# A two-layer diffusion backbone on one core: the heads' common rotary key is made in the Fourier block, and the second attention begins in another order

## The chip, the cores and the metric

The kernel runs on one core of a Trainium2 chip. The metric is the device time of one execution in microseconds (us). Before the change three runs took 3230.91, 3232.22 and 3234.19 us; the median is 3232.22 us. The core has five engines that work side by side: TensorE (PE, matmuls), VectorE (DVE), ScalarE (ACT), GpSimd (POOL) and SyncE (SP, which here issues all DMA transfers). Each runs its own list of instructions in order; they wait for each other through semaphores.

## The reference, cut to what matters

1024 latent tokens and 256 context tokens of width 1024 go through two layers. Layer 0 mixes tokens by a latent attention beside a Fourier mixing, layer 1 by a windowed attention beside pooling; each layer ends in a gated feed-forward part. The change touches the two attentions only.

```
# layer 0: 12 heads; a key is 64 own numbers and 32 that all heads share
kv = (rmsnorm(ckv, ckv_g) @ w_ukv).reshape(B, L, 12, 64 + 64)
k  = concat([kv[..., :64], broadcast(k_rope[:, :, None, :])])   # k_rope: 32 rows, common to the heads
k  = rope_tail(rmsnorm(k, k_g), cos, sin)                       # rotation of the last 32
o  = latent_dense_attention(q, k, v, k_ctx, v_ctx, scale)
y  = concat([o, fourier_mix(h[..., A_IN:], w_f)]) @ w_out
# layer 1: 12 query heads in 4 groups, one key head per group, window of +-128, context keys in full
q = apply_rope(rmsnorm(q, q_g)); k = apply_rope(rmsnorm(k, k_g))   # the context keys are not rotated
o = window_attention(q, k, v, k_ctx, v_ctx, sink, scale)
```

## The kernel before, in words

Everything is kept transposed: features on the 128 partitions, the 1280 tokens (1024 latent, then 256 context) along the free axis, worked in chunks of 512, 512 and 256 (`CH`). The program is a row of blocks; at the end of a block all engines meet, and the next one starts together. No scheduler reorders anything: the order on each engine is that of the code.

**The Fourier block** (`latents_and_fourier`, L1396 to L1574). SP loads the Fourier tables and the value weights (L1419 to L1422). ACT and PE make the norms of the latents (L1436 to L1444, L1468), DVE makes the sums and differences of the Fourier input (L1537, L1539) and scales the latents (L1557, three instructions). PE then does the short Fourier stage (L1482 to L1495), waits for L1557 (`u` 3 at L1500), does the long one (L1504, L1505), some small pieces (L1508 to L1521), and 20 products for the values (L1530), which ACT takes out of the accumulation memory PS one by one (L1452).

**The first attention** (`heads0`, L1576 to L2113) begins with a preparation that only depends on things that the Fourier block has. SP loads the rotation table `rope` (L1684) into two tiles of `H` that held the Fourier input, and the first two heads' weights (L1688). POOL clears the rows 0 to 63 of the scratch `sk` (L1701), clears the unused rows 96 to 127 of eight operand buffers (L1704: `kh`, `kl`, `qh`, `ql`, two of each), sets a row of ones in each `kh` (L1707) and copies the first head's values (L1712). The common rotary key: ACT copies its 32 rows into `sk` (L2003), PE multiplies them with the rotation matrix (L1897), DVE scales the key by the table (L2088), multiplies PE's result by the other half of the table (L2092) and adds the two into `kx` (L2095), and ACT squares the key for the norms (L2006). PE's list waits for the table, for L2095 and for L2006 before head 0 is prepared: project (L1818, L1822), squares (L1834), norm (L1940, L1943 on ACT, L2027 on DVE), split into a high and a low half (L1951, L2061), cast (L1720 on POOL), row maxima (L1863, L2077) and the row of negated maxima (L1874, L1965). Then the scores of head 0 start (L1750), and from there on each head's preparation is woven into the head before it.

**The second attention** (`heads1`, L2232 to L2862) goes through five products per group of heads (`prods`: which of the two operand tiles and which chunk of tokens). Each product runs through these kinds of steps, placed in slots by `plan`: `sq` (ACT L2668), `nt` (PE L2593, L2595; ACT L2680, L2683), `tn` and `ro` (DVE, L2779, L2801 to L2807, or L2795 alone for a context chunk), `hi` (ACT L2692), `lo` (DVE L2815), `ca` (POOL L2500, the cast to bf16). `upfront` lays out the first four products, before any head. After `hi`, `lo` and `ca` SP moves pieces to the partitions where the matmuls want them (L2465 for the high half, L2471 for the cast one, L2474 for the low half). The row maxima of the first head (PE L2613 to L2618, DVE L2825, 8 of them) wait for the moved casts of three products, then come L2832, L2628 and the row copy L2697, and then the first scores (L2541). POOL's list begins with 13 clearings of unused rows (L2485 to L2491), SP's product loop waits for all of them, and so do POOL's casts.

## Time and profile before

| what | value |
|---|---|
| median of three runs | 3232.22 us |
| the profiled execution | 3230.8 us |
| its span | 3229.0 us |
| PE busy | 3072.0 us, 95% of the span |
| DVE, ACT, POOL busy | 50%, 33%, 15% |
| HBM traffic over the span | 50 GB/s |

The span runs from the first to the last instruction in the trace. All other times below are read from the same execution, in us from the start of the span. A row of the timeline gives the start, the duration, the engine, the line and the operation, then what is written and read; "x4" means four instructions of one kind put in one row, and a bracket behind it gives how long the engine was idle before and what released it. In the rows by stretch, PEclk is the clock that TensorE was granted as a share of 2.4 GHz (0.50 is 1.2 GHz).

### The profile page before, as it was taken

To read this page: it belongs to the slowest core of one execution; us is meant where nothing else is said; L and a number is where in the kernel's file an instruction comes from. 1 tells how busy PE (TensorE), PEld (TensorE's weight loads), DVE (VectorE), ACT (ScalarE), POOL (GpSimd) and SP (SyncE) were. 2 spreads that over 40 slices of the span, in tenths; PEclk is the share of its full clock that TensorE was granted. 3 is DMA by queue.
4 is the path that set the end of the run, shared out by engine and by line. 5 is a ranking of instruction groups with operands and counts; after the bars stand their busy time and mean duration, and the time that the engine had idled before them with its cause. 6 is when DMAs were issued, how large, how long until landed. Compare 5 with 4: busy or idle time off the path is not lost. (4 is left out here: it accounts for less than half of the span.)

```text
span 3229.0 us, 38657 instructions
## 1 busy us (share of the span) xinstructions
PE 3072.0 (95%) x14498; PEld 2201.1 (68%) x14498; DVE 1625.8 (50%) x2090; ACT 1062.7 (33%) x1519; POOL 479.9 (15%) x369
## 2 busy tenths in 40 slices
PE   5987999999999999999999998969999999999999
PEld 2553444444488888888888886844457788888887
DVE  5123556556436544555444456246654655554555
ACT  3013665665624211121222223026652322212221
POOL 0002555555600000000000010034540000000000
PEclk9997999999999999999999999989999999999999
DMA  9910000000031011101111101123211111111111
GB/s 377 365 38 17 4 3 3 3 2 2 7 117 47 33 39 39 39 32 39 39 39 39 39 14 40 39 62 75 58 41 46 60 46 50 61 39 45 45 60 57
DMA packets 49668, 177.68 MB, mean 55 GB/s; under 512 B 6354, under 2 KB 15826, under 8 KB 39763
## 3 DMA queue, kind: packets, MB, share of 16 engines
q1 hardware_dynamic: 49586, 176.59, 16.1%
q8 instruction: 52, 0.85, 0.1%
q14 instruction: 30, 0.24, 0.0%
HBM read 156.77 MB, written 4.19 MB: 50 GB/s over the span
## 5 line engine op out<-in xcount | busy, mean ns | idle before, releaser
L1022 PE MATMUL PS<-s_uh,f_Wh 128*128 128x512 f32 (+1 forms) x1760 | 493.6, 371 | 7.6 <-PEq L134 5.4
L1022 PE MATMUL PS<-s_uh,f_Wl 128*128 128x512 f32 (+1 forms) x1760 | 492.1, 370 | 0.0
L1022 PE MATMUL PS<-s_ul,f_Wh 128*128 128x512 f32 (+1 forms) x1760 | 491.8, 370 | 0.0
L1277 DVE SCALAR_TENSOR_TENSOR X<-PS,mod,X 128x512 f32<-128x512 f32 (+1 forms) x440 | 304.4, 697 | 288.5 <-PE PS L1022 288.3
L1022 PEld LDWEIGHTS PS<-s_uh,f_Wh 128*128 128x128 f32 x1760 | 309.4, 188 | 69.2 <-issue 6.2
L1022 PEld LDWEIGHTS PS<-s_ul,f_Wh 128*128 128x128 f32 x1760 | 309.5, 188 | 58.5 <-issue 0.2
L1022 PEld LDWEIGHTS PS<-s_uh,f_Wl 128*128 128x128 f32 x1760 | 309.3, 188 | 58.7
L1022 PE MATMUL PS<-f_gh,f_WDh 128*128 128x512 f32 (+1 forms) x880 | 329.8, 375 | 8.6 <-DVE X L1277 4.5
L1022 PE MATMUL PS<-f_gl,f_WDh 128*128 128x512 f32 (+1 forms) x880 | 324.6, 369 | 0.0
L1022 PE MATMUL PS<-f_gh,f_WDl 128*128 128x512 f32 (+1 forms) x880 | 324.5, 369 | 0.0
L1248 DVE SCALAR_TENSOR_TENSOR part<-PS,part,part 128x1023 f32<-128x1023 f32 (+1 forms) x129 | 127.0, 1012 | 290.5 <-ACT part L1148 290.4
L1155 ACT ACTIVATE part<-part 128x1280 f32<-128x1280 f32 (+1 forms) x44 | 51.4, 1168 | 621.8 <-DVE part L1255 621.8
L1148 ACT ACTIVATE part<-PS,part 128x1024 f32<-128x1024 f32 (+1 forms) x87 | 113.3, 1303 | 385.3 <-PE PS L1022 385.3
L1730 POOL TENSOR_TENSOR X<-X 128x1024 f32<-128x1024 f32 x96 | 229.5, 2390 | 59.6 <-ACT X L1974 58.7
L1022 PEld LDWEIGHTS PS<-f_gh,f_WDh 128*128 128x128 f32 x880 | 166.3, 189 | 42.9 <-DVE X L1277 8.8
L1974 ACT ACTIVATE X<-PS 128x512 f32<-128x512 f32 x252 | 146.1, 594 | 143.0 <-PE PS L1752 134.8
L1022 PEld LDWEIGHTS PS<-f_gl,f_WDh 128*128 128x128 f32 x880 | 166.6, 189 | 27.8 <-issue 0.2
L1022 PEld LDWEIGHTS PS<-f_gh,f_WDl 128*128 128x128 f32 x880 | 166.4, 189 | 27.4
L2077 DVE TENSOR_REDUCE part<-PS 128x1 f32<-128x512 f32 (+1 forms) x312 | 161.9, 580 | 13.9 <-PE PS L1863 13.1
L509 POOL TENSOR_TENSOR part<-part,part 128x512 f32<-128x512 f32 x7 | 9.4, 1338 | 1037.6 <-ACT part L499 1036.9
L1236 DVE TENSOR_TENSOR f_Wl<-part,f_Wh 128x1024 fp32r<-128x1024 f32 x85 | 103.9, 1222 | 98.4 <-ACT f_Wh L1137 98.4
L1781 PE MATMUL PS<-X,part 128*64 128x512 f32 x480 | 138.1, 614 | 0.0
(289 smaller groups left out, 4669.4 us busy)
## 6 DMA issues: line engine op xcount, KB each, us to landing
part<-in_mod_w SPq DMA_DIRECT2D x48, 1024.0 KB, 7.3
part<-in_w_up SPq DMA_DIRECT2D x88, 512.0 KB, 3.6
part<-in_w_down SPq DMA_DIRECT2D x22, 1024.0 KB, 5.5
part<-in_w_in SPq DMA_DIRECT2D x16, 512.0 KB, 4.7
part<-in_w_out SPq DMA_DIRECT2D x16, 512.0 KB, 3.6
h_qh<-h_stage_h SPq DMA_DIRECT2D x48, 128.0 KB, 2.4
X<-in_xT SPq DMA_DIRECT2D x4, 1280.0 KB, 9.6
X<-in_xT SPq DMA_DIRECT2D x8, 640.0 KB, 8.8
```

Source lines behind the costliest of these rows:

```text
L509: dve.tensor_tensor(self.acc[:, lo:hi], self.acc[:, lo:hi], self.sq[i % 2][:, lo:hi], ALU.add)\
L1022: mm = pe.matmul(ps(bank, x_.shape[-1]), w_, x_, start=first and p_ == 0, stop=final and p_ == 2)
L1148: op = act.activation((cg, cv)[kind][:, lo:hi], hidden(before, place, lo, hi), ACT.Identity, scale=cw[:, ds(f, 1), 1], bias=cw[:, ds(f, 1) ...
L1155: act.activation(sg[:, :], cg[:, :], ACT.Silu).then_inc(s["silu"], 1)
L1236: dve.tensor_tensor(Wl[place % 2][:, :, :], W[place % 2][:, :, :], Wh[place % 2][:, :, :].bitcast(F32), ALU.subtract).then_inc(s["lo"], 1)
L1248: op = dve.scalar_tensor_tensor(out=x[:, lo + 1:hi], in0=h[:, 0:hi - lo - 1], scalar=cw[:, ds(f, 1), 0], in1=x[:, lo + 1:hi], op0=ALU.mult ...
L1277: dve.scalar_tensor_tensor(out=X[:, m, lo:hi], in0=ps(bank, hi - lo), scalar=moda(layer, 5, m, 0 if lo < SEQ else 1), in1=X[:, m, lo:hi], ...
L1730: op = pool.tensor_tensor(ac[:, 0:SEQ], ac[:, 0:SEQ], p[:, :], ALU.add)
L1781: mm = pe.matmul(ps(OB, BANK, slice(64 * c, 64 * c + 64)), vs[b][:, u, :], p[:, c * BANK:(c + 1) * BANK], start=(u == 0), stop=(u == 9))
L1974: act.activation(pr[u % 3][:, i % 2 * BANK:i % 2 * BANK + BANK], ps(i % 3, BANK), ACT.Exp, scale=A_SCALE).then_inc(s["P"], 1)
L2077: dve.reduce_max(mc[:, r:r + 1], ps(MB[c], hi - lo), AX_X).then_inc(s["mc"], 1)
```

## The change

Four things are changed, all in the two attentions and the Fourier block.

1. The common rotary key is made in the Fourier block. SP loads the table there, once the Fourier input in `H` is used up (after the two waits for `eo` and `ab`), and issues the first two heads' weights; POOL clears `sk` there; ACT's copy and square, PE's rotation and DVE's products stand there, the products cut into a latent and a context piece, since PE now writes banks 6, 7 and 4. PE waits for the result (`krc`) before the context pieces and before the value products.
2. The clearing of unused rows for the first attention is split: POOL does the four buffers of head 0 and one row of ones, DVE the four of head 1 and the other one, at the start of DVE's list.
3. In the second attention, the context chunk is the second product of a group instead of the third, and `upfront` puts a product's `hi`, `lo` and `ca` right behind its `ro`, ahead of the next product's norms. Three of the eight row maxima of the first head stand ahead of the fourth product's `ro`, and wait for the casts of two products only.
4. POOL clears the five bf16 buffers first, and the others between its casts; SP's loop no longer waits for the clearings.

```diff
 # Fourier block
+ sp: for b in range(2): sp.dma_start(WQ[b], a["wqk0"][b:b + 1]...).then_inc(loaded[b], 16)
+     sp.wait_ge(s["eo"], 6)
+     sp.wait_ge(s["ab"], 7)
+     sp.dma_start(ROPE[0:A_QK], a["rope0"]).then_inc(s["tab"], 16)
+ act: act.activation(SK[64:96, :], H[0:32, 3, :], ACT.Copy).then_inc(s["kr"], 1)
+      act.wait_ge(s["krm"], 1)
+      act.wait_ge(s["krt"], 1)
+      act.activation(SK[64:96, :], H[0:32, 3, :], ACT.Square).then_inc(s["krs"], 1)
  pe:  pe.wait_ge(s["abc"], 7)
       pe.wait_ge(s["u"], 3)
+      for lo, hi in CH:
+          bank = 6 + lo // BANK if lo < SEQ else 4
+          mm = pe.matmul(ps(bank, hi - lo, slice(0, A_QK)), rot0[:, 1, :], SK[0:A_QK, lo:hi], ...)
       pe.wait_ge(s["df"], 32)
...
+      pe.wait_ge(s["krc"], 2)        # ahead of the context pieces, and again ahead of the values
 # first attention
  pool:
-     pool.memset(sk[0:64, :], 0.0).then_inc(s["zero"], 1)
-     for n, x in enumerate((*kh, *kl, *qh, *ql)):
+     for n, x in enumerate((kh[0], kl[0], qh[0], ql[0])):
+ dve: for n, x in enumerate((kh[1], kl[1], qh[1], ql[1])):
+          dve.memset(x[96:P, :].bitcast(F32), 0.0).then_inc(s["pad1"], 1)
+      dve.wait_ge(s["pad1"], 4)
+      dve.memset(kh[1][96:97, :].bitcast(F32), 1.0).then_inc(s["one1"], 1)
 # second attention
-     prods = [(0, 0), (0, 1), (0, 2), (1, 0), (1, 1)]
+     prods = [(0, 0), (0, 2), (0, 1), (1, 0), (1, 1)]
+     def piece(w, *after):
+         for kind, v in after + (("ro", w),) + (("tn", w + 1),) * (w < 3) + (("hi", w), ("lo", w), ("ca", w)):
+             at(UPFRONT, 0, kind, 0, v)
+     for w in range(3):
+         piece(w, ("sq", w + 1))
+         at(UPFRONT, 0, "nt", 0, w + 1)
+     first(range(3))
+     piece(3)
+     first(range(3, 8))
  sp:
-     sp.wait_ge(s["one"], 2 + QS)
...
-     if q > 1:
+     if q > 0:
          sp.wait_ge(s["rounded"], rounded(q + 1))
+     if q > 1:
          sp.wait_ge(s["moved"], moved(q + 1))
```

How the lists of the engines stand, before and after. First PE. Before, its list goes from the last pieces of the Fourier block over the block's end (the two branches) to the rotation of the common key:

```order
L1521 MATMUL PS<-part_1159,part_1154 128x256 x8
L1530 MATMUL PS<-part_1150,part_58 128x384 x20
L1411 UNCONDITIONAL_BRANCH
L1746 UNCONDITIONAL_BRANCH
L1897 MATMUL PS<-X,rot 96x512 x2
L1897 MATMUL PS<-X,rot 96x256
L1818 MATMUL PS<-part_58,part_1444 64x512 x2
L1834 MATMUL PS<-X,cst 96x512
```

After, the rotation (now L1523) stands in the Fourier block, behind the short Fourier stage (L1513 is its last piece) and ahead of the long one (L1529, L1530):

```order
L1507 MATMUL PS<-part_1155,part_58 128x256 x4
L1513 MATMUL PS<-part_1155,part_58 1x128 x2
L1523 MATMUL PS<-X,rot 96x512 x2
L1523 MATMUL PS<-X,rot 96x256
L1529 MATMUL PS<-part_1159,part_1156 128x512
L1530 MATMUL PS<-part_1159,part_1156 128x512
```

Three matmuls have moved past the long Fourier stage, the context pieces and the values; the first attention's list now begins with the first projections.

Second, VectorE around the same block's end. Before, `L1557` are the latents' scalings, `L1566` to `L1573` the Fourier results, then the block's end, the key (L2088 to L2095), and head 0's first product:

```order
L1557 SCALAR_TENSOR_TENSOR part_58<-part_58,sml,PS 128x1280 x3
L1566 TENSOR_TENSOR part_57<-PS,part_1156 128x512
...
L1411 UNCONDITIONAL_BRANCH
L2018 UNCONDITIONAL_BRANCH
L2088 SCALAR_TENSOR_TENSOR X<-X,sml,part_58 32x1280
L2092 TENSOR_TENSOR PS<-PS,part_58 32x1280
L2095 TENSOR_TENSOR X<-X,PS 32x1280
L2027 TENSOR_TENSOR PS<-X,PS 96x512
```

After, the same key work is L1590 to L1600, head 0's first product is L2045:

```order
L1590 SCALAR_TENSOR_TENSOR X<-X,sml,part_58 32x1280
L1595 TENSOR_TENSOR PS<-PS,part_58 32x1024
L1595 TENSOR_TENSOR PS<-PS,part_58 32x256
L1600 TENSOR_TENSOR X<-X,PS 32x1024
L1600 TENSOR_TENSOR X<-X,PS 32x256
...
L2036 UNCONDITIONAL_BRANCH
L2104 MEMSET h_kh_1471 32x1280
L2104 MEMSET h_kl_1473 32x1280
L2104 MEMSET h_qh_1467 32x1280
L2104 MEMSET h_ql_1469 32x1280
L2106 MEMSET h_kh_1471 1x1280
L2045 TENSOR_TENSOR PS<-X,PS 96x512
```

The key is behind the scalings, and five clearings stand ahead of head 0's first product.

Third, ScalarE at the start of the second attention (L2668 squares, L2680 and L2683 the inverse norm, L2692 the high half, which releases the cast, L2697 the row). Before:

```order
L2668 ACTIVATE part_7876<-part_7876 128x2x256
L2680 ACTIVATE X<-PS,eps 128x2x256
L2683 ACTIVATE PS<-X 128x512
L2668 ACTIVATE part_9015<-part_7876 128x512
L2680 ACTIVATE X<-PS,eps 128x2x256
L2683 ACTIVATE PS<-X 128x512
L2692 ACTIVATE h_stage_h_9026<-PS 128x512
L2668 ACTIVATE part_7876<-part_7876 128x256
L2680 ACTIVATE X<-PS,eps 128x256
L2683 ACTIVATE PS<-X 128x256
L2692 ACTIVATE h_stage_h_9028<-PS 128x512
```

After (L2709, L2721 with L2724, L2733):

```order
L2709 ACTIVATE part_7873<-part_7873 128x2x256
L2721 ACTIVATE X<-PS,eps 128x2x256
L2724 ACTIVATE PS<-X 128x512
L2709 ACTIVATE part_9012<-part_7873 128x256
L2733 ACTIVATE h_stage_h_9023<-PS 128x512
L2721 ACTIVATE X<-PS,eps 128x256
L2724 ACTIVATE PS<-X 128x256
L2709 ACTIVATE part_7873<-part_7873 128x2x256
L2733 ACTIVATE h_stage_h_9025<-PS 128x256
L2721 ACTIVATE X<-PS,eps 128x2x256
```

The first high half stands ahead of the second product's inverse norm, and the second product is the short one.

## Rows read from the trace of the kernel before

**Rows 1.** The page: busy time, share of the span and instructions of an engine.

```profile
PE 3072.0 (95%) x14498; PEld 2201.1 (68%) x14498; DVE 1625.8 (50%) x2090; ACT 1062.7 (33%) x1519; POOL 479.9 (15%) x369
```

**Rows 2.** Stretches: length, then busy PE, PEld, DVE, ACT, POOL; PEclk, DMA share, GB/s.

```profile
221.40:226.70 5.30, 5.25 (x6) 2.19 (x7) 0.00 (x0) 0.00 (x0) 0.00 (x0) 0.50 0.00 0
268.20:288.20 20.00, 13.52 (x17) 3.94 (x18) 5.73 (x5) 6.00 (x11) 10.82 (x11) 0.50 0.14 34
289.00:302.00 13.00, 8.89 (x25) 3.35 (x23) 8.46 (x13) 8.24 (x18) 1.62 (x3) 1.00 0.04 11
2119.40:2155.70 36.30, 17.64 (x52) 6.97 (x52) 19.49 (x28) 10.25 (x18) 15.26 (x17) 0.67 0.44 112
2160.00:2395.00 235.00, 222.82 (x1303) 109.91 (x1301) 144.12 (x192) 144.84 (x259) 123.45 (x117) 0.99 0.25 57
```

**Rows 3.** Timeline: the Fourier block's end, the first attention's start.

```profile
264.27 0.49 ACT L1452 ACTIVATE part<-PS 128x384 f32<-128x384 f32 x1 [0.16 <-PE PS L1530]
265.01 0.33 SPq L1684 DMA_DIRECT2D part<-in_rope  x1
...
271.50 4.58 PE L1897 MATMUL PS<-X,rot 96*96 96x512 f32 x6 [7.26 <-DMA part<-in_rope]
...
276.12 1.50 DVE L2092 TENSOR_TENSOR PS<-PS,part 32x1280 f32<-32x1280 f32 x1 [3.10 <-PE PS L1897]
277.72 1.49 DVE L2095 TENSOR_TENSOR X<-X,PS 32x1280 f32<-32x1280 f32 x1
...
279.26 3.68 PE L1818 MATMUL PS<-part,part 128*64 128x512 f32 x4 [3.18 <-DVE X L2095]
...
286.34 0.69 DVE L2027 TENSOR_TENSOR PS<-X,PS 96x512 f32<-96x512 f32 x1 [7.13 <-ACT PS L1943]
```

**Rows 4.** Timeline: the Fourier block's middle.

```profile
215.86 0.60 PE L1495 MATMUL PS<-part,part 128*1 128x128 f32 x4
...
216.91 4.44 DVE L1557 SCALAR_TENSOR_TENSOR part<-part,sml,PS 128x1280 f32<-128x1280 f32 x3
...
221.45 2.05 PE L1504 MATMUL PS<-part,part 128*128 128x512 f32 x2 [4.99 <-issue]
...
240.87 0.69 DVE L1566 TENSOR_TENSOR part<-PS,part 128x512 f32<-128x512 f32 x1 [19.52 <-ACT part L1448]
```

**Rows 5.** POOL's clearings, grouped, 265 to 280 us: count, busy us, mean ns.

```profile
L1704 POOL MEMSET h_kh<- 32x1280 f32 x2 | 2.3, 1160 | 0.1
```

**Rows 6.** DMA issues: count, KB each, median us from issue to landing.

```profile
part<-in_rope SPq DMA_DIRECT2D x1, 960.0 KB, 6.4
part<-part SPq DMA_DIRECT2D x4, 64.0 KB, 2.0
```

**Rows 7.** Timeline: the second attention's start.

```profile
2124.94 0.70 DVE L2807 TENSOR_TENSOR PS<-X,PS 128x512 f32<-128x512 f32 x1
...
2128.26 0.69 ACT L2680 ACTIVATE X<-PS,eps 128x512 f32<-128x512 f32 x1 [3.87 <-PE PS L2595]
2128.90 3.62 POOL L2491 MEMSET h_ql<- 64x1024 f32 x4
...
2129.52 0.58 ACT L2692 ACTIVATE h_stage_h<-PS 128x512 fp32r<-128x512 f32 x1
...
2134.08 2.07 PE L2593 MATMUL PS<-part,cst 128*128 128x512 f32 x2 [2.93 <-ACT part L2668]
...
2137.89 0.69 ACT L2680 ACTIVATE X<-PS,eps 128x512 f32<-128x512 f32 x1 [3.87 <-PE PS L2595]
...
2144.06 0.54 SPq L2471 DMA_DIRECT2D part<-part  x1
...
2145.93 0.40 PE L2613 MATMUL PS<-part,part 128*128 128x256 bf16 x1 [8.07 <-DMA part<-part]
...
2155.79 0.77 PE L2541 MATMUL PS<-h_qh,h_ks 128*128 128x512 f32 x1 [1.15 <-issue]
```

**Rows 8.** DVE's part of the first head's maxima, grouped, 2145.5 to 2154 us.

```profile
L2825 DVE TENSOR_REDUCE part<-PS 128x1 f32<-128x640 f32 (+1 forms) x8 | 6.2, 790 | 3.4 <-PE PS L2618 3.3
```

More of the change, by code:

```diff
@@ L1591, in heads0 @@
             vs = [take(10, 64) for _ in range(2)]
-            wq = [take(256) for _ in range(2)]
-            Xf = X[:, :, :].rearrange("p k n -> p (k n)")
+            assert o == O_A + 8 * T + 20 * 64
+            o += 512
+            wq = WQ
             acc = [Xf[:, n * T:(n + 1) * T] for n in range(2)]
@@ L1596, in heads0 @@
             rest = 2 * T + 6 * BANK
-            kx, sk = [Xf[:, rest + n * T:rest + (n + 1) * T] for n in range(2)]
+            kx, sk = KX, SK
             rest += 2 * T
@@ L2114, in program @@
         input_and_mods(norm00, u0, copy_take(H, T))
-        latents_and_fourier()
+        loaded = [sem(f"h0_w{b}") for b in range(2)]
+        latents_and_fourier(loaded)
         source0 = Source("out0_", 0, a["w_out0"], T, MIX, [k * T for k in range(KT)],
@@ L2322, in plan @@
                 for jj, r in enumerate((-8, -2, 4)):
[L2323 to L2324 removed]
+                    if (G, jj) == (0, 0):
+                        continue
+                    if (G, jj) == (0, 1):
+                        maxima(G, jj, EARLY, 4)
                     else:
@@ L2518, in casts, with keys, queries_pad @@
                                 cast(*what)
-                    casts(UPFRONT, 0)
+                    def keys(b):
+                        pool.memset(kh[b][64:P, :].bitcast(F32), 0.0).then_inc(s["zero"], 1)
+                        pool.wait_ge(s["zero"], b + 1)
+                        pool.memset(kh[b][64:65, :].bitcast(F32), 1.0).then_inc(s["one"], 1)
+                    def queries_pad(n):
+                        pool.memset(ql[n][64:P, :].bitcast(F32), 0.0).then_inc(s["one"], 1)
+                    for x in (kb[0], qb[2], qb[0], qb[1], kb[1]):
+                        pool.memset(x[64:P, :], 0.0).then_inc(s["pad"], 1)
+                    pool.wait_ge(s["pad"], 2 + C_GROUP)
+                    for kind, *what in steps(UPFRONT, 0):
+                        if kind == "ca":
+                            w = what[1]
+                            cast(*what)
+                            pool.wait_ge(s["cast"], w + 1)
+                            if w == 0:
+                                keys(0)
+                            elif w < 3:
+                                queries_pad(w - 1)
+                            if w < 3:
+                                pool.wait_ge(s["one"], w + 1)
+                    queries_pad(2)
+                    queries_pad(3)
+                    keys(1)
+                    pool.wait_ge(s["one"], 2 + QS)
+                    pool.wait_ge(s["pad"], 2 + C_GROUP)
                     for n in range(C_HEADS):
```

123 lines of the change are left out of this document (58 added, 65 removed).

## The prediction, written before the changed kernel ran

> **What bounds the kernel now.** I read the page first: PE is busy for 3072.0 us, 95% of the span [rows 1]. So a change that only shifts work between the other engines is worth something only where PE stands still, and what is worth reading is the stretches in which it does. The busy times by stretch give two of them that the change touches. From 268.2 to 288.2 us PE is busy for 13.5 of 20.0 us, and at half clock; from 2119.4 to 2155.7 us for 17.6 of 36.3 us [rows 2]. The body of the second attention has PE busy for 222.8 of 235.0 us [rows 2], little to win. Then I read the timeline of both stretches for what PE waits for.
>
> *The first attention's start.* The last value product is taken out by ACT at 264.27 us for 0.49 us, and SP issues the rotation table at 265.01 us [rows 3]. The table holds 960 KB and lands 6.4 us later [rows 6]. The rotation on PE waits for it, 7.26 us idle, until 271.50 us, and takes 4.58 us; then DVE's L2092 and L2095 take 1.50 and 1.49 us in sequence, and PE's first projection starts at 279.26 us, after another 3.18 us idle [rows 3]. From the block's start to the first projection are 279.26 - 265.01 = 14.25 us in which nothing of head 0 is done.
>
> *The second attention's start.* PE is last idle for 8.07 us, released at 2145.93 us by the DMA of the third product's cast, issued at 2144.06 us; the first scores start at 2155.79 us [rows 7]. The first product is finished by DVE at 2124.94 + 0.70 = 2125.64 us, but ACT makes its high half only at 2129.52 us, since the second product's inverse norm (2128.26 us) stands before it in ACT's list; and POOL, which casts it, is clearing buffers until 2128.90 + 3.62 = 2132.52 us [rows 7]. So everything that is moved is some 7 us late from the first product on.
>
> **Part 1: the key moves (saves 14.1, costs 2.2).** What goes: with the key and the weights ready, PE projects at once when the block starts. It starts when SP does, 265.01 us, plus about 0.1 us for the first wait; the gap that goes is 279.26 - 265.15 = 14.1 us.
>
> What comes into the Fourier block, engine by engine:
> - PE: three matmuls between the short and the long stage, after the wait for DVE's scalings, which ends at 221.45 us [rows 4]. In the first attention the same three take 4.58 us, at half clock [rows 2, 3]. Here the clock is also 0.50 from 221.4 to 226.7 us, while PE is fully busy [rows 2]; after 5.3 us of work it is back at full speed. I take that this slow time stays as long, so that the long stage has its slow part shortened by what the rotation takes of it. Then the three cost what they do at full clock, half of about 4.3 us: 2.2 us. The bounds are 0 (hidden, if PE had waited for something later anyway; nothing shows it) and 4.6 us (the slow time starts anew).
> - SP: the table can be issued when the short stage has used up its input, at 215.86 + 0.60 = 216.5 us [rows 4]; plus 6.4 us it lands at 222.9 us. The two weight loads go out behind the Fourier tables and are not wanted before 265 us.
> - DVE: behind the scalings (216.91 + 4.44 = 221.35 us) it now waits for the table, then scales, and from 226 us, when PE's rotation is out, does the products: 1.5 + 1.5 + 1.5 us, and some 0.2 us for the two cuts. It is done by 230 us. What is queued behind is L1566 at 240.87 us, before which DVE is idle for 19.52 us [rows 4]. Hidden with 10 us to spare.
> - ACT: copy and square are 1.3 us each and lie in the same idle time; POOL has nothing else. Nothing.
> - The waits for `krc` on PE, ahead of the context pieces and the values, are past by 230 us.
>
> So 14.1 - 2.2 = 11.9 us.
>
> **Part 2: clearings split between POOL and DVE (about even).** POOL's clearings are 1160 ns each [rows 5]. Four, then a row of ones, and head 0's values: POOL is done with the four 4.8 us after the block's start, in time for the first high half, which comes 7.8 us after the first projection before (286.34 + 0.7 - 279.26). The five on DVE are new and ahead of its first product L2027. No such DVE clearing is in this trace. Bounds: nothing, if they are short; above, the 1.50 us of L2092 over the same 32 x 1280 elements [rows 3], times five, 7.5 us. The nearest row is POOL's 1.16 us; I take 1.3 us, 6.5 us in all, DVE free some 6.6 us after the start. L2027 was wanted 286.34 - 279.26 = 7.1 us after the first projection. But PE now projects and squares at full clock, having been busy until just before, where the first projection and the first squares ran at 0.50 [rows 2]: that brings L2027 forward by about 1.7 us, to 5.4 us. The clearings hold it until 6.6 us. What remains of the clock's gain is 0.5 us. With both bounds the term is +1.7 us (gain) to -0.4 us.
>
> The Trainium skill ("VectorE: DVE Perf Modes", the section that zero memsets can be issued as uint32) says that a memset takes one cycle per element whatever the type; at DVE's 0.96 GHz, which the Trainium skill's "SBUF — State Buffer" gives ("SBUF: two separate sides"), that is an estimate of 1.33 us each. With it the sum would be the same within 0.2 us. No row here shows it.
>
> **The clock after that.** Before, PE ran at 1.00 from 289 to 302 us although it was busy for only 8.9 of 13.0 us, and fell afterwards [rows 2]. After, the thin stretch begins some 3 us sooner relative to the last dense work. The clock may fall within it; the 8.9 us of PE work would then take up to twice as long, partly beside ACT and DVE. I cost that at nothing and keep 4 us in the range.
>
> **Part 3: the second attention's start (saves 5.0).** I follow the new lists with the durations of the old ones. The first product is done at 2125.64 us as before. Now ACT makes its high half at once (until 2126.3 us). POOL has five clearings before, at most 1.16 us each, from 2119.4: done by 2125.2 us, so the cast starts at 2126.3 us instead of behind 2132.52 us. ACT goes on with the short context product (inverse norm about 0.9 us) and the third one's square (0.6 us): PE's norms of the third product start at 2127.8 us. From there to ACT's inverse norm are 3.8 us (2134.08 to 2137.89 us [rows 7]): 2131.6 us. Inverse norm 0.7 and 0.6 us, square 0.6 us: the fourth norms start at 2133.6 us and end at 2137.4 us. PE is then free for the maxima. Their casts: SP has eight issues of about 0.6 us for product one and two before the second cast, so from 2126.4 us it issues that one at 2132.7 us and it lands 2.0 us later [rows 6], at 2134.7 us. It isn't last; PE is. The first maximum starts at 2137.4 us against 2145.93 us, 8.5 us sooner. Against that, the fourth product's three DVE steps (2.1 us), high half (0.6 us) and low half (0.7 us) now stand between the third and the fourth maximum, where before they were done ahead of all: about 3.5 us. The rest, five more maxima, the negation and the row, is as long as before (eight reductions are 6.2 us with 3.4 us between [rows 8]). So 8.5 - 3.5 = 5.0 us: scores at 2150.8 us. POOL has to have cleared everything by then: fourth cast until 2144.1 us, two clearings of 0.9 and two of 1.16 us, 2148.3 us. That cover is 2.5 us thick. Bounds: 2 us, if SP's issues or POOL delay the third product; 8 us, if PE's norms find a full clock, as 0.67 on average [rows 2] leaves possible.
>
> In groups 1 to 3 the exchange of the second and third product delays the chunk of 512 by nothing that PE waits for: at 3.3 us per pair of key tiles (235.0 us [rows 2] over 12 heads of 6 pairs, less the first), its cast is placed nine pairs before its group and its first maximum six pairs before, 10 us later.
>
> **The sum.** 11.9 + 0.5 + 5.0 = 17.4 us. The profiled execution took 3230.8 us (span 3229.0 us and 1.8 us around it), so 3213.4 us; the median of the runs is 1.4 us above it, so 3214.8 us, in round numbers 3215.
>
> **The rivals.**
> - *A, 59%: as above*, 3212 to 3218 us.
> - *B, 20%: PE's clock falls in the thin stretch of head 0's preparation.* For it: before, it was low from 268 to 288 and again after 302 us, the same kind of work. Against: it stayed up from 289 to 302 us. Price 2 to 4 us, so 17.4 - 3 = 14.4: 3218 us.
> - *C, 9%: SP becomes what the second attention's start waits for.* The high halves now ask for SP early and its issues (0.6 us each, 21 up to the third product's end) and its added wait for the first two casts form a queue; the third product's casts come 3 us late. For it: PE's last release before was a DMA. Against: the cast of the third product has 3 us of cover. Saving 12.4 + 2 = 14.4 us: 3218 us; with more maxima held, 3220 us.
> - *D, 8%: clearings on DVE and POOL hold each other.* They run at the same moment and take 5 x 1.16 + 5 x 1.3 = 12.3 us in sequence instead of 6.5 us. L2027 then comes 12.3 instead of 6.6 us after the start, 5.7 us lost: 11.7 us saved, 3220.5 us. The trace has L2095 beside the clearings of POOL, each at its usual length [rows 3, 5], which speaks against it. The Trainium skill ("SBUF — State Buffer", the section "SBUF: two separate sides") says that an operation of DVE that uses both ports and one of GpSimd take a common pair of ports in turns, for a whole instruction; by that rule the time is this one. No row here has two clearings at once.
> - *E, 2%: slower.* The exchange of the chunks in groups 1 to 3: the product of 512 columns comes one place later, its eight issues of SP (5 us) land behind the fourth maximum, and PE stands still there. It decides from 10 us of delay per group on, the slack above; to eat 17.4 us it would need 6 us of standing PE in each of three groups: 3233 us and more, up to 3240 us.
> - *F, 2%: no change*, if the block's start is bound by something else that the table's wait hid, such as the first weights; they are loaded 70 us ahead, so I see no way: 3229 us.
>
> **Range and chances.** Range 3209 to 3223 us: the low end has the 1.7 us of part 2 and the 8 us of part 3, the high end B and D together with C. 0.2%, about what a measurement of this kernel tells from none, is 6.5 us. Cases A to D are faster by more than that: 96%. F within: 2%. E slower: 2%.
>
> **What would show it right or wrong.** In the profile after: the rotation's three matmuls at about 221.4 us and the long stage's end 2.2 us later; PE's first projection within 0.3 us of the block's start, near 267.3 us; five DVE clearings before the first product, which shows their length and whether POOL's stay at 1.16 us; head 0's first scores 12 us sooner. In the second attention the first maximum 18 us after the block's start instead of 26.6 us, a gap between the third and fourth, and the first scores 31.4 us after it instead of 36.4 us. Wrong would be an idle time of PE ahead of the context pieces or values (`krc` late), DVE still in its clearings at 7 us, or PE waiting for a DMA at the first or the fourth maximum.

## The result, and the profile after

The changed kernel takes 3211.2 us (median of four runs, 3209.98 to 3213.91), the kernel before 3233.0 us beside it (four runs, 3230.91 to 3234.19): ratio 0.9936, 95% interval 0.9924 to 0.9948. The profiled execution took 3211.42 us (span 3209.6), 19.4 us less than the profiled one of before; the medians are 21.8 us apart. 17.4 us less were forecast, and a time of 3215 us.

The page's engine line and the busy times by stretch, as in [rows 1] and [rows 2]:

```profile
PE 3064.2 (95%) x14498; PEld 2199.4 (69%) x14498; DVE 1632.6 (51%) x2097; ACT 1063.0 (33%) x1519; POOL 474.3 (15%) x364
```

```profile
222.60:227.90 5.30, 5.29 (x8) 2.27 (x9) 2.25 (x2) 0.70 (x1) 0.00 (x0) 0.51 0.00 0
268.20:275.00 6.80, 6.32 (x14) 1.79 (x14) 5.47 (x5) 3.50 (x6) 6.49 (x6) 1.00 0.00 1
275.00:277.40 2.40, 0.03 (x1) 0.06 (x1) 1.53 (x3) 1.49 (x4) 0.65 (x2) 1.00 0.00 0
277.40:285.60 8.20, 5.36 (x14) 1.97 (x14) 5.20 (x9) 5.72 (x12) 1.01 (x2) 1.00 0.00 0
285.60:302.00 16.40, 11.94 (x22) 3.23 (x22) 11.98 (x22) 4.14 (x9) 1.62 (x3) 0.51 0.03 9
```

In these rows, 0.51 and 0.50 are TensorE's half clock of 1.2 GHz and 1.00 its full one of 2.4 GHz. Head 0's preparation now begins at full clock and ends at half; before, half clock came first and full clock from 289 to 302 us.

The timeline of the Fourier block's middle, which answers to [rows 4] (and its rotation to the L1897 of [rows 3]):

```profile
217.69 0.33 SPq L1432 DMA_DIRECT2D part<-in_rope  x1
218.06 4.44 DVE L1584 SCALAR_TENSOR_TENSOR part<-part,sml,PS 128x1280 f32<-128x1280 f32 x3
222.61 4.55 PE L1523 MATMUL PS<-X,rot 96*96 96x512 f32 x6 [5.00 <-issue]
223.60 1.54 DVE L1590 SCALAR_TENSOR_TENSOR X<-X,sml,part 32x1280 f32<-32x1280 f32 x1 [1.09 <-DMA part<-in_rope]
226.95 1.46 PE L1529 MATMUL PS<-part,part 128*128 128x512 f32 x2
...
228.87 1.56 DVE L1600 TENSOR_TENSOR X<-X,PS 32x1024 f32<-32x1024 f32 x2
...
244.01 0.69 DVE L1605 TENSOR_TENSOR part<-PS,part 128x512 f32<-128x512 f32 x1 [13.58 <-ACT part L1466]
```

The rotation takes the slow 4.55 us that the long stage's beginning had before, and the long stage starts near full clock. DVE has finished the key by 230.4 us and then stands still for 13.58 us; the table came 5.9 us after its issue, by the row that answers to [rows 6]:

```profile
part<-in_rope SPq DMA_DIRECT2D x1, 960.0 KB, 5.9
```

The first attention's start, as [rows 3] and [rows 5]:

```profile
268.22 1.16 POOL L1739 MEMSET h_kh<- 32x1280 f32 x1 [72.17 <-POOLq L1416]
268.26 1.90 PE L1853 MATMUL PS<-part,part 128*64 128x512 f32 x4 [0.83 <-PEq L1416]
268.55 1.12 DVE L2104 MEMSET h_kh<- 32x1280 f32 x1 [15.12 <-PEq L1416]
...
269.89 1.12 DVE L2104 MEMSET h_kl<- 32x1280 f32 x1 [0.21 <-issue]
...
272.41 0.60 ACT L1968 ACTIVATE PS<-part 96x512 f32<-96x512 f32 x1
...
274.03 1.12 DVE L2106 MEMSET h_kh<- 1x1280 f32 x1 [0.33 <-DVE h_ql L2104]
...
275.18 0.69 DVE L2045 TENSOR_TENSOR PS<-X,PS 96x512 f32<-96x512 f32 x1
...
277.37 0.64 PE L1869 MATMUL PS<-X,cst 96*96 96x256 f32 x2 [2.39 <-DVE h_kl L2079]
...
286.19 1.99 PE L1869 MATMUL PS<-X,cst 96*96 96x512 f32 x2 [0.93 <-issue]
```

PE projects 0.04 us after the block's start. The norm that DVE's product wants is there at 272.41 + 0.60 = 273.01 us; DVE is in its clearings until 275.15 us, 2.1 us too long, and PE then waits 2.39 us. At 286.19 us the norm matmuls of head 0's last product take 1.99 us, where the same ones of its first product, at 270.56 us, took 1.10 us: the clock has fallen.

The second attention's start, as [rows 7]; its block starts at 2109.50 us:

```profile
2116.56 0.61 POOL L2516 CAST part<-h_stage_h 128x512 bf16<-128x512 f32 x1 [2.08 <-ACT h_stage_h L2733]
...
2123.55 1.12 PE L2634 MATMUL PS<-part,cst 128*128 128x512 f32 x2 [1.96 <-ACT part L2709]
...
2125.38 0.27 PE L2654 MATMUL PS<-part,part 128*128 128x256 bf16 x1
...
2129.46 0.69 DVE L2848 TENSOR_TENSOR PS<-X,PS 128x512 f32<-128x512 f32 x1
2129.86 0.39 PE L2654 MATMUL PS<-part,part 128*128 128x256 bf16 x1 [2.63 <-DMA part<-part]
...
2138.20 0.77 PE L2582 MATMUL PS<-h_qh,h_ks 128*128 128x512 f32 x1 [1.15 <-issue]
```

The first maximum is 15.9 us after the block's start (before 26.6), the first scores 28.7 us (before 36.45). The fourth product's norm matmuls at 2123.55 us take 1.12 us where the same product's in [rows 7] took 2.07. The DMA of the third product's cast releases the fourth maximum, but this wait costs nothing: DVE is busy with the fourth product's rotation until 2130.15 us, then with its low half, and takes up the fourth reduction only at 2131.42 us, when PE has been done with that maximum for 0.6 us. The eight reductions, as [rows 8], are as long as before and wait less:

```profile
L2866 DVE TENSOR_REDUCE part<-PS 128x1 f32<-128x640 f32 (+1 forms) x8 | 6.0, 787 | 1.2 <-PE PS L2659 1.0
```

### The profile page after: what moved, and what is told of

Read it like the earlier page. It is cut to its first block and busy times, and to the rows that moved or that the text cites. A ratio compares the mean times of both kernels' runs of the same rounds, so it can differ in the third digit from the quotient of the medians.

```text
span 3209.6 us, 38659 instructions
## 1 busy us (share of the span) xinstructions
PE 3064.2 (95%) x14498; PEld 2199.4 (69%) x14498; DVE 1632.6 (51%) x2097; ACT 1063.0 (33%) x1519; POOL 474.3 (15%) x364
## 5 line engine op out<-in xcount | busy, mean ns | idle before, releaser
L1022 PE MATMUL PS<-s_uh,f_Wh 128*128 128x512 f32 (+1 forms) x1760 | 493.7, 371 | 7.6 <-PEq L134 5.4
L1022 PE MATMUL PS<-s_ul,f_Wh 128*128 128x512 f32 (+1 forms) x1760 | 492.0, 370 | 0.0
L1022 PE MATMUL PS<-s_uh,f_Wl 128*128 128x512 f32 (+1 forms) x1760 | 491.9, 370 | 0.0
L1022 PEld LDWEIGHTS PS<-s_uh,f_Wh 128*128 128x128 f32 x1760 | 309.3, 188 | 69.4 <-issue 6.2
L1022 PEld LDWEIGHTS PS<-s_uh,f_Wl 128*128 128x128 f32 x1760 | 309.4, 188 | 58.8
L1022 PEld LDWEIGHTS PS<-s_ul,f_Wh 128*128 128x128 f32 x1760 | 309.4, 188 | 58.4 <-issue 0.2
L1022 PE MATMUL PS<-f_gh,f_WDh 128*128 128x512 f32 (+1 forms) x880 | 329.6, 375 | 8.4 <-DVE X L1277 4.3
L1022 PE MATMUL PS<-f_gl,f_WDh 128*128 128x512 f32 (+1 forms) x880 | 324.7, 369 | 0.0
L1022 PE MATMUL PS<-f_gh,f_WDl 128*128 128x512 f32 (+1 forms) x880 | 324.6, 369 | 0.0
L1022 PEld LDWEIGHTS PS<-f_gh,f_WDh 128*128 128x128 f32 x880 | 166.2, 189 | 42.6 <-DVE X L1277 8.7
L1022 PEld LDWEIGHTS PS<-f_gl,f_WDh 128*128 128x128 f32 x880 | 166.5, 189 | 27.8 <-issue 0.2
L1022 PEld LDWEIGHTS PS<-f_gh,f_WDl 128*128 128x128 f32 x880 | 166.5, 189 | 27.5
L2095 DVE TENSOR_REDUCE part<-PS 128x1 f32<-128x512 f32 (+1 forms) x312 | 161.9, 580 | 13.9 <-PE PS L1898 13.1
```

The lines of the kernel that those rows point to most:

```text
L1022: mm = pe.matmul(ps(bank, x_.shape[-1]), w_, x_, start=first and p_ == 0, stop=final and p_ == 2)
L2095: dve.reduce_max(mc[:, r:r + 1], ps(MB[c], hi - lo), AX_X).then_inc(s["mc"], 1)
```

## The experiments

The landmarks that I compare, in us: the start of DVE's three latent scalings; from there to head 0's first projection; from that to head 0's first scores; from those to the second attention's block start; from that to its first scores; from those to the first matmul of the output part; the rest of the span. Each row is one profiled execution.

| kernel | scalings | to projection | to scores | to block 2 | to its scores | to output | rest |
|---|---|---|---|---|---|---|---|
| before | 216.9 | 62.35 | 40.17 | 1799.9 | 36.45 | 251.6 | 821.6 |
| changed | 218.1 | 50.20 | 41.93 | 1799.3 | 28.70 | 250.3 | 821.2 |
| e1 | 217.8 | 50.46 | 41.92 | 1799.9 | 36.47 | 251.8 | 821.5 |
| e2 | 216.1 | 62.25 | 40.16 | 1799.8 | 28.70 | 250.6 | 821.2 |
| e3 | 217.7 | 50.09 | 37.86 | 1801.5 | 30.76 | 250.1 | 821.1 |
| e4 | 219.7 | 45.75 | 40.16 | 1800.2 | 28.77 | 250.0 | 821.1 |
| e5 | 219.9 | 49.20 | 40.16 | 1801.9 | 32.59 | 248.6 | 822.5 |
| e6 | 215.5 | 50.18 | 41.93 | 1799.7 | 28.93 | 249.8 | 821.1 |
| e7 | 218.2 | 57.94 | 40.98 | 1799.6 | 35.81 | 250.1 | 821.2 |
| e8 | 217.0 | 50.20 | 37.86 | 1803.7 | 30.42 | 248.8 | 820.9 |
| e9 | 217.1 | 45.71 | 39.04 | 1801.3 | 28.67 | 250.1 | 821.1 |
| e10 | 216.9 | 50.22 | 41.92 | 1799.8 | 33.81 | 251.0 | 821.5 |
| e11 | 216.9 | 50.36 | 41.92 | 1799.8 | 28.64 | 250.1 | 821.2 |
| e12 | 219.0 | 50.09 | 37.85 | 1801.5 | 30.75 | 250.4 | 820.9 |

e1 to e4 ran beside runs of the kernel before with a median of 3231.7 us, e5 to e8 beside 3230.7, e9 to e12 beside 3230.3.

**e1, the first half alone.** The changed kernel with the second attention (`heads1`) of before; its Fourier block and first attention are the changed ones.

> The changed kernel with the second attention of before. Theory (the two parts are independent, and each takes away idle time of PE at its own place): the first attention's first projection 12 us sooner than before, counted from the long Fourier stage's start less its own wait, first scores 10.5 us sooner, the second attention's start as before (first scores 36.4 us after its block's start); in all 10 to 11 us faster than before (ratio 0.9967). Rival (most of the gain, and the 2 us that the two attentions' starts don't explain, comes from elsewhere, such as the exchanged chunks in groups 1 to 3): less than 8 us here, and more in the other half than the second attention's start shows.

3221.0 us (0.9966, 0.9954 to 0.9978), 10.7 us saved. The projection comes 11.9 us sooner against the scalings, the scores are then 1.75 us slower.

**e2, the second half alone.** The kernel before with the changed `heads1`.

> The kernel before with the second attention of the changed one. Theory: first scores of the second attention 28.7 us after its block's start instead of 36.4, all else as before: 8 to 9 us faster than before (ratio 0.9974). Rival (the exchange of chunks in groups 1 to 3 gives or takes time too): the body from the first scores to the block's end differs from before's by more than 1 us.

3221.3 us (0.9968, 0.9955 to 0.9981), 10.4 us saved: 7.75 us at the start, and 1.1 us more up to the output. 10.7 + 10.4 = 21.1 us against the whole change's 21.8 (3233.0 - 3211.2), or 20.5 against the 3231.7 us beside e1 and e2: the halves add up.

**e3, DVE's clearings behind head 0's first step.**

```diff
-     (DVE, before all steps) the four memsets of kh[1], kl[1], qh[1], ql[1], the row of ones
      steps(0, 0)
+     the same five memsets
      steps(1, 1)
```

PE accordingly waits for head 1's row of ones only ahead of head 1.

> The changed kernel with DVE's five clearings behind head 0's preparation, where DVE has nothing to do for 14 us, instead of ahead of it. Theory (the clearings hold head 0's first product for 2.1 us, from 273.0 to 275.2 us, and PE's idle time of 2.4 us behind it helps the clock to fall at 286 us): the first product 2.1 us sooner, the first scores 2 us sooner, 4 us if the clock stays up. In all 3207 to 3209 us against 3211. Rival (the high half waits for POOL's clearings of the same buffers anyway, or ACT's list is the longest): the first product is sooner, the first scores are not, 3211 us.

```profile
272.61 0.69 DVE L2044 TENSOR_TENSOR PS<-X,PS 96x512 f32<-96x512 f32 x1 [19.61 <-ACT PS L1967]
...
274.79 0.64 PE L1868 MATMUL PS<-X,cst 96*96 96x256 f32 x2 [0.24 <-DVE h_kl L2078]
```

3211.0 us (0.9936, 0.9922 to 0.9949), the same as the changed kernel. Yet at head 0's scores it is 4.07 us ahead (41.93 - 37.86): 2.1 us for the clearings (the product comes 4.78 instead of 6.92 us after the projection; PE waits 0.24 instead of 2.39 us), and the rest because the clock holds longer, until about 288.7 us, which is behind head 0's last norms (1.07 us at 283.62 us). That the missing hole is what holds the clock up is not shown: in e7, below, PE waited only 0.34 us at this point, and the last norms were slow all the same (1.99 us at 293.26 us). Then it loses 2.2 us before the second attention and 2.1 us in its start. In both, PE is at half clock where it was at full clock in the changed kernel: from the feed-forward part's first matmul (L1022, where PEq is PE's sequencer) on, then at the second attention's first norms.

```profile
992.96 0.77 PE L1022 MATMUL PS<-s_uh,f_Wh 128*128 128x512 f32 x1 [3.15 <-PEq L134]
...
2107.89 1.96 PE L2632 MATMUL PS<-part,cst 128*128 128x512 f32 x2 [2.78 <-ACT part L2707]
```

In the changed kernel the same two, behind the same waits:

```profile
997.48 0.47 PE L1022 MATMUL PS<-s_uh,f_Wh 128*128 128x512 f32 x1 [3.15 <-PEq L134]
...
2110.22 1.12 PE L2634 MATMUL PS<-part,cst 128*128 128x512 f32 x2 [2.78 <-ACT part L2709]
```

**e4, the latent chunks' rotation ahead of the wait for the last scaling.**

```diff
      pe.wait_ge(s["abc"], 7)
-     pe.wait_ge(s["u"], 3)
      for lo, hi in CH:
+         if lo == SEQ: pe.wait_ge(s["u"], 3)
```

> The changed kernel with the key's rotation of the two latent chunks ahead of PE's wait for DVE's scalings instead of behind it (the context chunk stays behind). Theory (PE stands idle there for 5.0 us, and the rotation costs 2.2 us behind it): the latent chunks run in the idle time, the long Fourier stage starts 3.4 us sooner relative to the wait's end and its end comes 1.7 us sooner; if PE's work in the gap also keeps the clock up, its first 5 us run in 2.6 us and it is 4 us. In all 3207 to 3209.5 us. Rival (the clock falls as before and its slow time is counted from the end of the wait): the gain is what four rows cost at full clock, 1.7 us, and no more; or nothing, if the long stage's slow time grows by what the rotation no longer takes of it.

```profile
219.78 1.96 PE L1524 MATMUL PS<-X,rot 96*96 96x512 f32 x4 [0.57 <-DVE part L1581]
224.15 1.17 PE L1524 MATMUL PS<-X,rot 96*96 96x256 f32 x2 [2.42 <-DVE part L1585]
225.11 1.91 PE L1530 MATMUL PS<-part,part 128*128 128x512 f32 x2
```

3207.5 us (0.9925, 0.9911 to 0.9938). Four of the rotation's six matmuls lie in PE's idle time, at full clock (1.96 us); the other two and the long stage's first products still run at half clock. The long stage begins 3.4 us sooner against the scalings, as the theory has it, and ends 2.8 us sooner. The projection comes 4.4 us sooner: the small pieces L1548 (L1547 in the changed kernel) take 5.21 instead of 6.36 us, at a better clock, which e5 below had too, without this edit, in 5.24 us. So some 3 of the 4.4 us are the edit's own; the rest goes by a clock that need not be the edit's doing. The profiled execution is 3.9 us shorter than the changed one. The medians differ by 3.7 us, and by 2.4 us when each is taken against the kernel before beside it (24.2 us saved against 21.8); the five runs (3204.8 to 3209.2) all lie below the changed kernel's four. The gain is there, at 2.4 to 3.7 us.

**e5, POOL's thirteen clearings first again.** POOL's list of before with the changed lists of all others.

> The changed kernel with one part undone: in the second attention POOL clears all thirteen buffers first and only then casts, as before; the lists of the other engines and SP's loop stay changed. My account of the second attention's start says that POOL's list has to be cut for the rest to count: in the changed kernel the first cast starts 7.0 us after the block's start (2116.56 us), behind five clearings; with thirteen it starts at about 13.2 us (in the kernel before they ended 2132.52 - 2119.34 = 13.2 us after it). Every cast then comes some 4 us late, the first maximum about 19.5 us after the block's start instead of 15.9, the first scores about 32.4 us instead of 28.7, total +3.7 us, about 3215. Rival: the order of ACT's and DVE's lists alone made the gain and the casts have slack; then the first scores stay within 0.5 us of 28.7 and the total is that of the changed kernel, 3211.

3216.0 us (0.9953, 0.9937 to 0.9968); first maximum 19.5 us after the block's start, first scores 32.6 us. The theory's numbers: the casts are on the path. One thing is mixed in: in this execution the first norms (L2619 below) ran at half clock, as in e3, and e3, whose casts were not late, had its first scores at 30.76 us. So the late casts cost 3.9 us against the changed kernel and 1.8 us against e3. PE does wait for a cast's DMA ahead of the first maximum, 1.66 us. POOL's clearings end 13.2 us after the block's start whatever PE's clock is, so I take the 3.9 us for their price at a full clock too; no run shows that alone.

This execution also shows something that was not asked. Up to the second attention its program is that of the changed kernel, but its scalings began 1.9 us later (219.9 against 218.1). The projection came 1.0 us sooner against them (the small pieces L1547 took 5.24 instead of 6.36 us), and head 0's scores 1.8 us sooner against the projection: the clock fell behind the 2.38 us for which PE waits there, at about 278.7 us, was back at 282.2 us and up at the matmul that was slow in the changed kernel (287.07 us below). Then 2.1 us (against e11) were lost before the second attention, with the same slow L1022 as in e3.

```profile
287.07 1.07 PE L1869 MATMUL PS<-X,cst 96*96 96x512 f32 x2 [0.93 <-issue]
...
996.82 0.76 PE L1022 MATMUL PS<-s_uh,f_Wh 128*128 128x512 f32 x1 [3.15 <-PEq L134]
...
2111.91 2.08 PE L2619 MATMUL PS<-part,cst 128*128 128x512 f32 x2 [2.78 <-ACT part L2694]
...
2130.70 0.28 PE L2639 MATMUL PS<-part,part 128*128 128x256 bf16 x1 [1.66 <-DMA part<-part]
```

**e6, all eight maxima behind the fourth product.** `first(range(3))` goes, `first(range(8))` stands behind `piece(3)`.

> The changed kernel with one part undone: all eight row maxima of the second attention's first head stand behind the fourth product's steps; in the changed kernel three stand ahead of them. In the changed kernel PE has 2.6 us between the third and the fourth maximum in which it waits for a DMA, and DVE does the fourth product's rotation there. Theory: the three maxima are hidden in the time in which DVE would wait for the fourth product's norm anyway, but their own reductions (0.8 us each) then only move behind; the end is set by the cast of the third product and by the DVE work in sequence, which is the same in both, so it costs about 0.4 us: first scores 29.1 us after the block's start. Rival: the three maxima ahead are worth their full length on PE and DVE, 2.2 us: first scores at 30.9 us and a total of 3213.

3213.0 us (0.9945, 0.9929 to 0.9960), not told from the changed kernel; first scores 28.9 us, 0.2 us later. The split of the maxima is worth next to nothing: DVE's rotation of the fourth product takes the time that the three reductions leave.

**e7, only the loads early.** The kernel before with the table's and the two weights' loads in the Fourier block.

> The kernel before, with only the loads moved: the rotation table and the first two heads' weights are loaded in the Fourier block, the common key is still made at the first attention's start. It tells how much of the gain of the key's move is the wait for the table and how much is the key's own work. In the kernel before PE waits 6.4 us there (265.15 to 271.50 us) for the table; PE's rotation (4.6 us at half clock), DVE's two products (3.0 us) and its start stay. Theory: the first projection comes 14.25 - 6.3 = 8.0 us after the block's start instead of 14.25, so 6.2 us of the 11.9 come from the table, 3226 us; if POOL's clearing of the scratch (row 0 to 63) or ACT's copy is late, up to 1.5 us less. By the clock: PE stands still for less long, so the rotation may run at full clock, 2.3 us more gain (5.7 us after the block's start, 3224). Rival: nearly all of the gain is the table's wait, first projection within 3 us of the block's start, 3221.

```profile
266.31 1.16 POOL L1708 MEMSET X<- 64x1280 f32 x1 [71.52 <-POOLq L1415]
267.50 1.27 ACT L2010 ACTIVATE X<-part 32x1280 f32<-32x1280 f32 x1 [1.46 <-POOL X L1708]
268.87 4.05 PE L1904 MATMUL PS<-X,rot 96*96 96x512 f32 x6 [3.35 <-ACT X L2010]
...
276.11 3.63 PE L1825 MATMUL PS<-part,part 128*64 128x512 f32 x4 [3.19 <-DVE X L2102]
```

3226.9 us (0.9992, 0.9982 to 1.0001): not told from the kernel before. Its ten runs scatter from 3223.4 to 3233.2 us; the four above 3231 us have a mean granted clock of 0.977 or 0.978, the others, the profiled one among them, 0.979 to 0.982. In the profiled execution the projection comes 9.8 us after the block's start, 4.4 us sooner than before. Behind the table's wait stood POOL's clearing and ACT's copy, 2.6 us in sequence; so in this profile 4.4 of the 14 us were the table and nearly 10 the key's own work, which only moving it hides. The rival, a projection within 3 us of the block's start and 3221 us, is refuted.

**e8, e3 with 2.6 us of delay ahead of the second attention.** The last two scalings of the pooling run twice on DVE.

> The kernel of e3 (DVE's clearings behind the first step of head 0), with the two last scalings of the pooling in layer 1 done twice on DVE. This puts about 2.6 us of delay ahead of the second attention and touches nothing in it. In e3 the second attention's first scores came 30.8 us after its block's start instead of 28.7, with PE's first norms at half clock, though its instructions there are the same as in the changed kernel. Theory (where the clock comes back depends on when the block starts against the clock's own time): with the start moved by 2.6 us the first scores come back to about 28.7 us, and the total is that of e3 plus only about 0.5 us. Rival (something in e3 itself makes that start slow): they stay at 30.8 us, and the total is e3 plus 2.6 us, 3213.6. A third outcome, another value between or beyond, would say that the clock there varies with the start, but not in the way I suppose.

3210.5 us (0.9939, 0.9925 to 0.9952), e3's time though 2.6 us of work were added; the block starts 2.2 us later against head 0's scores. The five runs scatter from 3209.1 to 3216.3 us, so the median doesn't settle what 2.6 us of delay cost. The first norms stayed slow and the first scores came at 30.4 us, so my forecast for them was wrong. The delay made PE's idle time before the norms 4.97 instead of 2.78 us, so it was no mere shift, and I can't separate the two. In the profile, 1.3 us came back in the body (248.8 against 250.1 us to the output), where I had looked for nothing; e5 has a body as short, but loses 1.4 us of it again in the rest.

**e9, e3 and e4 together.**

> The changed kernel with the edits of e3 and e4 together: DVE's clearings behind head 0's first step, and the latent chunks' rotation ahead of the wait for the last scaling. Alone, e4 gave 3207.5 us against 3211.2 and e3 3211.0. Theory: the two act at different places, and at the scores of head 0 their gains add as far as the clock lets them: head 0's scores came 42.2 us after the value products' end in the changed kernel, 38.2 in e3, 40.5 in e4; here 38 us at best, with the block starting 4.4 us sooner. Total 3203 to 3206 us if nothing is given back. Rival: what e3 showed, that the time gained in thin stretches is given back by PE's clock elsewhere (2 us at layer 0's feed-forward start, 2 us at the second attention's start): 3207 us, the same as e4.

3206.8 us (0.9929, 0.9915 to 0.9942): faster than the kernel before by 23.5 us. That is 1.7 us more than the changed kernel saved against its own runs of before; the one run of the changed kernel beside it (e11) took 3210.7 us, and e9's five runs scatter from 3203.3 to 3210.6 us. It is not told from e4 alone (24.2 us saved). The scores come 39.04 us after the projection, not 37.86, and 1 us more than in e4 goes before the second attention. The rival's total holds. Of its two places only one is slow here, L1022; the second attention's first norms are at full clock:

```profile
989.55 0.77 PE L1022 MATMUL PS<-s_uh,f_Wh 128*128 128x512 f32 x1 [3.15 <-PEq L134]
...
2103.81 1.12 PE L2633 MATMUL PS<-part,cst 128*128 128x512 f32 x2 [2.78 <-ACT part L2708]
```

**e10, the context third again.**

```diff
- prods = [(0, 0), (0, 2), (0, 1), (1, 0), (1, 1)]
+ prods = [(0, 0), (0, 1), (0, 2), (1, 0), (1, 1)]
```

> The changed kernel with one part undone: in the second attention the context chunk is again the third product of a group, not the second; every cast still stands right behind its rotation. It tells how much of the start's gain is the order of the products. Theory: the second cast now is that of a whole chunk of 512 with its norms ahead, and the third that of the context, so the first two maxima's operands come later on PE and ACT: first maximum about 20.4 us after the block's start instead of 15.9, first scores about 33 us instead of 28.7, total +4, 3215. Rival: the order is worth nothing, since all four products are wanted before the last maximum; first scores within 0.7 us of 28.7 and the total that of the changed kernel.

3217.8 us (0.9963, 0.9950 to 0.9976). First maximum 20.35 us, first scores 33.8 us after the block's start, 5.1 us later than in the changed kernel. So casting sooner alone is worth 36.45 - 33.8 = 2.6 us, the order the other 5.1, and with POOL's old list (e5) 3.9 of the 7.75 us are lost (of which the clock may hold a part): the parts need each other.

**e11 and e12, the changed kernel and e3 once more.**

> The changed kernel once more, for a second profile. It tells whether PE's clock in the thin stretches is a property of the kernel or of the execution. In its first profile the clock was back from about 2127.8 us at the second attention's start (first norms L2634 in 1.1 us at full clock), and the long Fourier stage began 226.95 us from the start. If the clock's pattern belongs to the kernel, the same instructions have the same lengths here, first scores 28.7 us after the block's start, and the landmarks agree within 0.5 us. If it belongs to the execution, the landmarks differ by up to 2 us at one or more of: scores of head 0, layer 0's feed-forward start, second attention's first scores.

> The kernel of e3 once more, for a second profile. In e3 PE's clock fell at layer 0's feed-forward start (2.2 us) and before the second attention's first norms (2.1 us, first scores 30.8 us after the block's start), and both were read as what ate its gain of 4 us. If they belong to the kernel, both are here again, with first scores at 30.8 us. If they belong to the execution, at least one of the two is absent here, first scores at 28.7 us, and the span is 2 to 4 us shorter than e3's 3209.2 us.

```profile
996.45 0.47 PE L1022 MATMUL PS<-s_uh,f_Wh 128*128 128x512 f32 x1 [3.16 <-PEq L134]
```

```profile
994.34 0.77 PE L1022 MATMUL PS<-s_uh,f_Wh 128*128 128x512 f32 x1 [3.15 <-PEq L134]
...
2109.14 1.96 PE L2632 MATMUL PS<-part,cst 128*128 128x512 f32 x2 [2.78 <-ACT part L2707]
```

3210.7 and 3212.3 us, one run each. Both kernels repeat their own pattern: 28.64 us after 28.70, 30.75 after 30.76, L1022 fast in the one and slow in the other. That is two profiles of each kernel. With e5 it reads: the same kernel can repeat its clock closely, but an execution that is 2 us off by the Fourier block had another pattern.

## Why the prediction was right, and where its terms were off

Where the 19.4 us of the profiled executions are, against the terms:

| stage | forecast | measured |
|---|---|---|
| part 1: to the projection | 11.9 | 12.15 |
| part 2 and the clock, to head 0's scores | 0.5 | -1.8 |
| to the second attention's block | 0 | 0.6 |
| part 3: its start | 5.0 | 7.75 |
| its body and close, the rest | 0 | 1.8 |
| before the scalings | 0 | -1.15 |

The sum is better than its terms. Part 3 gave 2.75 us more than forecast and the body and close 1.8 us that nobody forecast; part 2 with the clock gave 2.3 us less, and the scalings, whose start scatters from 215.5 to 219.9 us over the profiles, began 1.15 us later. That these cancel to within 2 us is luck.

**Part 1** held in each step: the gap gone, the rotation at the price of full clock because it stands in the slow time that the long stage had (the long stage begins 4.35 us later against the scalings, but ends only 1.9 us later, and the last value product is out 2.05 us later, 49.90 instead of 47.85 us after their start, where 2.2 was forecast), the key hidden with 13.6 us to spare. e1 gives 11.9 us. The row before the scalings is no effect: fourteen profiles have them between 215.5 and 219.9 us, and two of the changed kernel at 218.1 and 216.9.

**Part 2** is where a sign was wrong. The clearings were sized right: 1.12 us each, 1.34 us from start to start, DVE free 6.9 us after the start where I had 6.6. The estimate of 1.33 us that was worked out from the Trainium skill ("VectorE: DVE Perf Modes", "Zero memsets can be issued as uint32") fits the distance, not the duration. What failed is "That brings L2027 forward by about 1.7 us, to 5.4": at full clock the product's inputs were there 4.8 us after the start (273.01 us), so the clearings cost 2.1 us, not 1.2. And "I cost that at nothing", said of the clock, is rival B's step: the clock fell at about 285.9 us, before the norms of head 0's last product, instead of after 302 us. The stretch from projection to scores is 1.8 us longer than before where 0.5 shorter was forecast, so 2.3 us are missing. About 0.3 of them are the clearings: the first product starts 6.92 us after the projection, 0.2 us sooner than before instead of 0.5. The rest, 1.9 us, comes behind it and goes with B's mechanism, a little under its price of 2 to 4 us; against e5, whose clock was up again there, it is 41.93 - 40.16 = 1.8 us. I gave it 20%. Six profiles have this code up to that point: in five the clock is down at head 0's last norms (changed, e1, e6, e10, e11), in e5 it fell sooner and was back. In e3, without the 2.4 us hole, 4.07 us come back; what makes the clock fall where it does stays open.

**Part 3** had the mechanism and the order of its steps; its size was off by the clock. The first maximum was to come 18.0 us after the block's start and came at 15.9: the fourth product's norms ran at full clock, about 2.0 us from start to end (2123.55 to 2125.54 us) where I took the 3.8 us of [rows 7]. That is the bound of 8 us which I named, and it was nearly the value. From the first maximum to the scores I had 3.5 us more than before and it was 3.0. The casts (e5, 3.9 us) and the order (e10, 5.1 us) both carry it; the split of the maxima (e6) next to nothing. One count in the working was off: ahead of the second cast stand ten issues of SP, not eight; they took 6.36 us (2116.45 to 2122.81 us), and the 6.3 us that the sum used are right. A further 1.8 us appear in the body and behind it (1.4 in e2), for which I had no term. They belong to the second attention's lists, since e1, with the old ones, has none of it (251.8 and 821.5 us); no experiment was made on what they are.

**The rivals.** C: PE did wait for a DMA at the fourth maximum, 2.63 us, which I had named as a sign of being wrong; it cost nothing, since DVE was not ready for this maximum before 2131.42 us, so the sign was badly chosen. The other sign, DVE in its clearings at 7 us, was missed by 0.1 us. D: refuted, DVE's and POOL's clearings ran side by side at 1.12 and 1.16 us. I had also misapplied the rule: the Trainium skill ("SBUF — State Buffer", "Who interferes with whom") says too that a DVE instruction with at most one SBUF input outside the two-port modes doesn't contend with GpSimd, and the rows agree. E: refuted, the body is no longer than before in any kernel with the new order. F: refuted by e1 and by PE's 0.04 us. The range's high end was said to hold B, C and D together; at their prices (3, 3 and 5.7 us) the three make 3226.5 us, so 3223 us held B and D only.

## What to carry to other kernels

Before hiding a wait, look at what stands in sequence behind it: here the table was 4.4 of 14 us, and the rest went only because the whole chain moved into another block's idle time. A piece that is moved should stand in a hole of the engine that it runs on, not behind it (e4, 2.4 to 3.7 us for one moved wait). A gain of 2 to 4 us ahead of thin stretches should be followed to the end of the program before it is believed, since PE's clock may take it back 700 and 1800 us later (e3).

## What the runs showed of the hardware

The same matmuls behind the same idle time ran at either clock, by when they came: L1022 behind 3.15 us of idle in 0.47 or 0.77 us, the first norms of the second attention behind 2.78 us in 1.12 or 1.96 us, in kernels whose programs differ only far ahead of them. Each such place is worth some 2 us. The two don't go together: e9 has L1022 slow and the norms fast. e5 shows that it isn't the program alone: unchanged up to the second attention, and 1.9 us later in the execution, it had other clocks at L1547 (5.24 against 6.36 us), in head 0's preparation and at L1022. The Trainium skill ("TensorE: Matmul & The Clock Gate", Part 1) says that the chip's measuring of PE's activity runs freely and isn't started by the kernel, so that a change of clock depends on where the work lands in it; e5 against the changed kernel is in line with this; it is one execution. A simple account, that a shift alone brings the fast pattern back, failed in e8. What decides which pattern a place gets stays open.
